# Attention phase of a two-layer decoder trunk: scores three head pairs ahead, turned rows in their own PSUM banks, a new order within each step

## The reference, cut to what matters

```python
D_MODEL, SEQ, HEAD_DIM, N_Q_HEADS, N_KV_HEADS, WINDOW, BLOCK = 1024, 4096, 64, 16, 4, 128, 128

# swa_sink_attention: blocks of 128 queries, each against its own and the preceding 128 keys
s = einsum('bnqkgd,bnjkd->bnkgqj', q, kb)              # q already scaled by HEAD_DIM ** -0.5
s = where(mask, s, -inf)                               # band of 128 keys
m = maximum(max(s, axis=-1), sink)
e = exp(s - m)
pr = e / (sum(e, axis=-1) + exp(sink - m))
o = einsum('bnkgqj,bnjkd->bnqkgd', pr, vb).reshape(B, S, N_Q_HEADS * HEAD_DIM)
h = h + o @ w_o
hn = rmsnorm(h, g_ffn[1])                              # rows for the experts
logits = hn @ [w_group_router, w_expert_router]        # 4 + 32 columns
```

## Time and profile before

| | |
|---|---|
| median of three runs | 5489.29 us |
| profiled execution, its own time | 5481.81 us |
| span of its trace | 5479.8 us |
| attention, first to last copy of `qT` | 2647.8 to 3562.2 us of the span |
| TensorE busy over the span | 4717.2 us (86%) |
| VectorE busy over the span | 2947.2 us (54%) |

### The profile page before, as it was taken

The page is one execution under the profiler, slowest core; times in us unless marked ns, Lnnn a source line. Parts: engine busy times, 40 slices in busy tenths (PEclk is TensorE's granted clock), DMA queues, the critical chain, the costliest instruction groups (busy, mean ns, idle before and its releaser), DMA issues. The chain is left out here.

```text
span 5479.8 us, 90667 instructions
## 1 busy us (share of the span) xinstructions
PE 4717.2 (86%) x29473; PEld 2996.9 (55%) x29893; DVE 2947.2 (54%) x5970; ACT 1945.8 (36%) x2841; POOL 1559.3 (28%) x1159
## 2 busy tenths in 40 slices
PE   7928999999938999998588888845999999986898
PEld 6916766666623444443355555524766676653444
DVE  5664444444444544443577777773444444435665
ACT  6714444433322122221344444413434344322232
POOL 1114444443401111110232333304444344322232
PEclk9959999999969999999799999967999999998999
DMA  6729999998945555553555555518999999854443
GB/s 219 273 96 316 308 308 302 302 295 285 288 139 143 147 146 143 153 146 93 130 146 153 149 148 151 140 46 277 307 309 304 297 310 282 289 162 150 146 137 114
DMA packets 1163421, 1129.77 MB, mean 206 GB/s; under 512 B 859984, under 2 KB 871248, under 8 KB 1163344
## 3 DMA queue, kind: packets, MB, share of 16 engines
q1 hardware_dynamic: 1117264, 961.02, 57.8%
q0 software_dynamic: 46080, 167.79, 9.4%
HBM read 695.58 MB, written 227.54 MB: 168 GB/s over the span
## 5 line engine op out<-in xcount | busy, mean ns | idle before, releaser
L724 POOL TENSOR_TENSOR ex_w_lo<-ex_raw,ex_w_hi 128x2048 bf16<-128x2048 f32 x192 | 779.2, 4085 | 1161.8 <-ACT ex_w_hi L778 1161.8
L778 ACT ACTIVATE ex_w_hi<-ex_raw 128x2048 bf16<-128x2048 f32 x384 | 707.3, 1900 | 523.4 <-PE ex_ps_y L110 187.9
L875 PE MATMUL ex_ps_gate<-ex_xT,ex_w_hi 128*128 128x0 bf16 x2048 | 572.3, 280 | 161.6 <-DMA ex_xT<-ex_xrow 126.3
L876 PE MATMUL ex_ps_gate<-ex_xT,ex_w_hi 128*128 128x0 bf16 x2048 | 572.1, 280 | 0.0
L877 PE MATMUL ex_ps_gate<-ex_xT,ex_w_lo 128*128 128x0 bf16 x2048 | 571.6, 279 | 0.0
L875 PE MATMUL ex_ps_up<-ex_xT,ex_w_hi 128*128 128x0 bf16 x2048 | 558.6, 273 | 0.0
L876 PE MATMUL ex_ps_up<-ex_xT,ex_w_hi 128*128 128x0 bf16 x2048 | 558.3, 273 | 0.0
L877 PE MATMUL ex_ps_up<-ex_xT,ex_w_lo 128*128 128x0 bf16 x2048 | 558.1, 273 | 0.0
L857 DVE COPY ex_y<-ex_ps_y 128x512 f32 x324 | 224.1, 692 | 566.5 <-PE ex_ps_y L110 515.6
L841 DVE TENSOR_TENSOR ex_aT<-ex_silu,ex_ps_up 128x384 bf16<-128x384 f32 x256 | 141.8, 554 | 719.6 <-PE ex_ps_up L877 538.2
L109 PE MATMUL ex_ps_y<-ex_w_lo,ex_aT 128*128 128x512 bf16 x1296 | 492.2, 380 | 8.5
(11 more groups left out here) (310 smaller groups left out, 9071.8 us busy)
## 6 DMA issues: line engine op xcount, KB each, us to landing
ex_raw<-in_w_exp_gate SPq DMA_DIRECT2D x128, 1024.0 KB, 11.1
ex_raw<-in_w_exp_up SPq DMA_DIRECT2D x128, 1024.0 KB, 13.8
ex_raw<-in_w_exp_down SPq DMA_DIRECT2D x128, 1024.0 KB, 5.8
y_rows<-ex_y SPq DMA_DIRECT2D x162, 512.0 KB
cb_hin<-h_mid SPq DMA_DIRECT2D x64, 512.0 KB, 4.7
mix_x<-in_x SPq DMA_DIRECT2D x32, 512.0 KB, 4.6
h_mid<-mix_h SPq DMA_DIRECT2D x32, 512.0 KB, 5.2
y_rows<-mix_zeros SPq DMA_DIRECT2D x32, 512.0 KB, 5.9
```

Of the source, the lines that this page charges most:

```text
L724: eng.tensor_tensor(w_lo[u][:, w], raw[:, c, :], w_hi[u][:, w], ALU.subtract).then_inc(lo_done, 1)
L778: act.activation(w_hi[u][:, c * WCHUNK:(c + 1) * WCHUNK], raw[:, c, :], ACT.Copy).then_inc(hi_done, 1)
L875: pe.matmul(out, hi, x_hi, start=j == 0, stop=False)
L876: pe.matmul(out, hi, x_lo, start=False, stop=False)
```

## The change: what it does

Times of issue are moved in all five lists; arithmetic, instruction counts and shapes stay.

- `scores`, `top`, `exps` are issued three pairs ahead (c + 3) in place of two. `ps_s` still has two halves.
- A new tile `ps_t` of two PSUM banks takes the turned queries, the turned `hn` rows and the logits. `ps_x` is left to the projection. The turned keys move to bank 0 of `ps_o`. `qT` is doubled.
- Queries and keys of tile s+1 are turned in slot 1 (before: slot 6).
- Square, scaling, power and `hn`: scaling and power of tile s-2 now stand in slot 0 and `hn` in slot 1 of step s (before: slots 6 and 7 of step s-1). Its PE transposes stand in slot 3, the copy `hnT` in slot 3, the router in slot 7.
- `project(0,0)` moves from slot 1 to slot 0, `project(1,0)` from 2 to 1, `project(.,1)` from 3 and 4 to 4 and 5.
- `over(s+1, 0)` moves ahead of the `top`s of slot 7; `rests` stood ahead of `over` in every slot already.
- SyncE: the `hrow` store moves from slot 1 to 5, the K/V load from 3 to 5, the `h4` store from 6 to 7.

```diff
-        qT = m.sb("qT", [P, NP, P])
+        qT = [m.sb(f"qT{u}", [P, NP, P]) for u in (0, 1)]
-        ps_log, ps_k = ps_o[:, 0, 0:NLOG], ps_o[:, 1, 0:2 * P].rearrange("p (j n) -> p j n", j=2)
+        ps_t = m.ps("t", [P, D])
+        ps_log, ps_k = ps_t[:, 0:NLOG], ps_o[:, 0, 0:2 * P].rearrange("p (j n) -> p j n", j=2)
...
 ScalarE
-                    if c < NP - 2 and cur:
-                        exps(s, c + 2)
+                    if c < NP - 3 and cur:
+                        exps(s, c + 3)
+                    if c >= NP - 3 and nxt:
+                        exps(s + 1, c + 3 - NP)
+                    if c == 1 and nxt:
+                        act.wait_ge(turn_mm, s + 2)
+                        wait(act, s_mm, NP * s)
+                        act.activation(qT[v][:], ps_t[:], ACT.Copy).then_inc(qT_done, 1)
+                    if c == 1 and prev2:
+                        act.wait_ge(hn_done, s - 1)
...
                         act.activation(hrow[u][:, 0:D], hn[:], ACT.Copy).then_inc(hi_done, 1)
                     if c == 2 and prev:
                         out_hi(s - 1, 1)
...
+                    if c == 3 and prev2:
+                        act.wait_ge(hnT_mm, s - 1)
...
+                        act.activation(hnT[:], ps_t[:], ACT.Copy).then_inc(hnT_done, 1)
+                    if c == 6 and cur:
+                        out_hi(s, 0)
                     if c == 6 and prev:
...
                         act.activation(junk[:], h4[v][:], ACT.Square, accum_out=ss[:]).then_inc(ss_done, 1)
...
 VectorE, after the change (rests, over as before)
                     if cur:
                         rests(s, c)
                     if c < NP - 1 and cur:
                         over(s, c + 1)
+                    if c == NP - 1 and nxt:
+                        over(s + 1, 0)
+                    if c == 0 and prev2:      # scaling of tile s-2
+                    if c == 1 and prev2:      # hn of tile s-2
+                    if c == 3 and prev:
+                        out_lo(s - 1, 1)
+                    if c == 4 and nxt:        # kT of tile s+1
+                    if c == 4 and cur:        # low part of the values
+                    if c == 3 and prev2:      # low part of hrow
+                    if c in (5, 6) and prev:
+                        residual(s - 1, v, c - 5)
+                    if c < NP - 3 and cur:
+                        top(s, c + 3)
+                    if c >= NP - 3 and nxt:
+                        top(s + 1, c + 3 - NP)
                     if c == 7 and cur:
                         out_lo(s, 0)
+                    if c == 7 and prev2:      # logits of tile s-2
...
 TensorE, after the change
+                    if c < NP - 3 and cur:
+                        scores(s, u, c + 3)
+                    if c == 5 and prev:
+                        project(1, 1).then_inc(wo_mm, 1)
+                    if c >= NP - 3 and nxt:
+                        scores(s + 1, v, c + 3 - NP)
+                    if c == 0 and prev:
+                        pe.wait_ge(ol_done, 2 * s - 1)
+                        wait(pe, h4_done, 2 * (s - 1))
+                        project(0, 0)
+                    if c == 1 and prev:
+                        project(1, 0)
+                    if c == 1 and nxt:        # turn queries into ps_t, keys into ps_k
+                    if c == 2 and prev:
+                        weigh(s - 1, v, 1)
+                    if c == 3 and prev2:      # turn hn into ps_t, after qT_done
+                    if c == 4 and prev:
+                        pe.wait_ge(ol_done, 2 * s)
+                        project(0, 1).then_inc(wo_mm, 1)
+                    if c == 6 and cur:
+                        weigh(s, u, 0)
+                    if c == 7 and prev2:      # router into ps_log
```

More of the change, by code:

```diff
@@ L1531, in step @@
                         turn(s, c)
-                    if c == 1 and prev2:
+                    if c == 5 and prev2:
                         sp.wait_ge(lo_done, s - 1)
                         sp.dma_start(row_t[s - 2], hrow[u][:]).then_inc(row_st[u], 16)
-                    if c == 3 and load:
+                    if c == 5 and load:
                         wait(sp, v_done, s + 1)
                         sp.dma_start(kv_in[u][:], kv_t[s + 2]).then_inc(kv_ld[u], 16)
-                    if c == 6 and prev:
+                    if c == 7 and prev:
                         sp.wait_ge(h4_done, 2 * s)
@@ L1562, in step @@
                 for c in range(NP):
[L1563 to L1566, removed]
                     if c < NP - 1 and cur:
@@ L1570, in step @@
                         heads(s + 1, 0)
+                    if c == 0 and prev2:
+                        pool.wait_ge(ms_done, s - 1)
+                        wait(pool, hn_done, s - 2)
+                        pool.tensor_tensor(rs[:], ms[:], C.minus_half[:], ALU.pow).then_inc(rs_done, 1)
             steps(pool, step)
@@ L1597, in step @@
                         act.activation(hrow[u][:, 0:D], hn[:], ACT.Copy).then_inc(hi_done, 1)
[L1598 to L1601, removed]
                     if c == 2 and prev:
                         out_hi(s - 1, 1)
-                    if c == 1 and cur:
+                    if c == 2 and cur:
                         act.wait_ge(kv_ld[u], done(s, u))
@@ L1609, in step @@
                         act.activation(vp[u][:, 0, :, :], vin, ACT.Copy).then_inc(vh_done, 1)
+                    if c == 3 and prev2:
+                        act.wait_ge(hnT_mm, s - 1)
+                        wait(act, log_mm, s - 2)
+                        act.activation(hnT[:], ps_t[:], ACT.Copy).then_inc(hnT_done, 1)
+                    if c == 6 and cur:
+                        out_hi(s, 0)
                     if c == 6 and prev:
                         act.wait_ge(h4_done, 2 * s)
-                        wait(act, ss_done, s - 1)
+                        wait(act, ms_done, s - 1)
                         act.activation(junk[:], h4[v][:], ACT.Square, accum_out=ss[:]).then_inc(ss_done, 1)
[L1614 to L1619, removed]
-                    if c < NP - 2 and cur:
-                        exps(s, c + 2)
-                    if c >= NP - 2 and nxt:
-                        exps(s + 1, c + 2 - NP)
             steps(act, step)
@@ L1678, in step @@
                 for c in range(NP):
-                    if c == 3 and prev:
-                        out_lo(s - 1, 1)
                     if cur:
@@ L1684, in step @@
                         over(s, c + 1)
[L1685 to L1696, removed]
+                    if c == NP - 1 and nxt:
+                        over(s + 1, 0)
+                    if c == 0 and prev2:
+                        dve.wait_ge(ss_done, s - 1)
+                        dve.tensor_scalar(ms[:], ss[:], 1.0 / D, EPS, ALU.mult, ALU.add).then_inc(ms_done, 1)
+                    if c == 1 and prev2:
+                        dve.wait_ge(rs_done, s - 1)
+                        wait(dve, hnT_mm, s - 2)
+                        dve.scalar_tensor_tensor(out=hn[:], in0=h4[u][:], scalar=rs[:, 0:1], in1=g_ffn[:],
+                                                 op0=ALU.mult, op1=ALU.mult).then_inc(hn_done, 1)
+                    if c == 3 and prev:
+                        out_lo(s - 1, 1)
+                    if c == 4 and nxt:
                         dve.wait_ge(turn_mm, s + 2)
@@ L1703, in step @@
                         last.then_inc(kT_done, 1)
[L1704 to L1714, removed]
+                    if c == 4 and cur:
+                        dve.wait_ge(vh_done, s + 1)
+                        vin = kv_in[u][:, KVW:2 * KVW].rearrange("p (j e) -> p j e", e=HEAD)
+                        dve.tensor_tensor(vp[u][:, 1, :, :], vin, vp[u][:, 0, :, :], ALU.subtract).then_inc(v_done, 1)
+                    if c == 3 and prev2:
                         dve.wait_ge(hi_done, s - 1)
@@ L1717, in step @@
                         dve.tensor_tensor(hrow[u][:, D:2 * D], hn[:], hrow[u][:, 0:D], ALU.subtract).then_inc(lo_done, 1)
+                    if c in (5, 6) and prev:
[4 more added lines that the diff above has]
+                        top(s + 1, c + 3 - NP)
                     if c == 7 and cur:
                         out_lo(s, 0)
[L1720 to L1724, removed]
+                    if c == 7 and prev2:
+                        dve.wait_ge(log_mm, s - 1)
+                        at = slice(s - 2, s - 1) if isinstance(s, int) else bass.ds(s - 2, 1)
+                        dve.tensor_tensor(C.logits[:, at, :].rearrange("p a b -> p (a b)"), ps_log, bias[:],
+                                          ALU.add).then_inc(log_done, 1)
             steps(dve, step)
@@ L1738, in scores @@
                 for b, keys in ((0, kT[1 - par]), (1, kT[par])):
-                    mm = pe.matmul(ps_s[:, c % 2, :, b * P:(b + 1) * P], qT[:, c, :], keys[:, jj, :, :],
```

(34 more changed lines are left out.)

4 lines of the change are left out of this document (1 added, 3 removed).

## The result

Four runs took 5327.07 to 5338.02 us, median **5332.57 us**; the kernel before, timed beside them, 5489.56. The ratio is 0.9716, 95% interval 0.9704 to 0.9728: 157 us faster, where 105 were forecast.

A forecast was written before the change was run, and what follows sets the result against it. TensorE is near its limit, VectorE second; a dependency circle of 26.0 us plus 0.4 for the clock gives steps of 26.4 against 29.9. Thirty steps save 105 us: 5384 us, range 5350 to 5440.

The forecast's parts named there:

- The wait for `hn` goes, the clock with it: TensorE's 2.8 us wait for `hn` ahead of its transposes goes; the clock's fall had cost 1.0 us a step.
- What is late next: `project(0,0)` in slot 0 waits about 2.2 us for `out_lo(s-1,0)`, at the end of a chain of 26.0 us.
- the circle: Chain from `project(0,0)` over scores, `top`, exponentials, `out_hi`, `out_lo`, slots 4 to 7 back to `project(0,0)`: 26.0 us.
- VectorE's own work, "a bare slot is ... in all 2.19": `rests` 0.79, `over` 0.25, `top` with `nmx` 1.15 make 2.19 us a slot; with the other work 23.9 a step.
- The clock, "I take 0.4": Clock falling at the new wait ahead of `project(0,0)` costs 0.4 us a step, within bounds of 0 and 2.6.
- TensorE's own work 23.85: Scores, `project`, `weigh`, router and transposes on TensorE sum to 23.85 us a step at 2.4 GHz.
- Filling and draining, "0, within 3": Steps outside the 30 counted have the same dependent chains: 0 us change, within 3 either way.
- Three ahead: `exps` gets over two slots before `over` wants it, where it had one, so VectorE's wait for it goes.
- SyncE: Moving the `hrow` store, K/V load and `h4` store costs 0, up to 1 us a step if a landing doubles.
- `over(s+1,0)`, "so 0": Moving it ahead of slot 7's last `top`s saves at most 1.15 us towards `heads`, 0 inside the loop.
- The exponentials' wait far below 9.7 us: Sign of being right: ScalarE's exponentials wait for `nmx` far below 9.7 us a step.
- A: Rival: TensorE runs through and the clock never falls, step 25.0 us at best, 5342 us; chance 0.13.

The follow-up runs named there:

- e4: Kernel before with only `hn` rows and logits given two PSUM banks of their own, `hn` turned in slot 2: 5384.22 us, 26.58 us a step.
- e2: Changed kernel with `out_lo(s,0)` moved from the end of slot 7 to behind `over` of the next slot 0: 5401.68 us, 27.30 us a step.
- e3: Changed kernel with `out_lo(s,0)` ahead of the last `top` of slot 7 and `out_hi(s,0)` ahead of slot 6's exponentials: 5312.13 us, 24.25 us a step.
- e9: Changed kernel with `residual(s-1,1)` in slot 7 in place of slot 6: 5333.66 us, 25.23 us a step in the mean.
- e10: Changed kernel with `over(s+1,0)` behind the last `top` of slot 7, as before the change: 5326.59 us, 24.88 us a step.
- e1: Changed kernel with `scores`, `top`, `exps` two pairs ahead in place of three, copy `kT` one slot later: 5407.40 us, 27.35 us a step.
- e7: Changed kernel with SyncE's order of `hrow` store, K/V load and `h4` store as before the change: 5329.21 us, 25.10 us a step.
- e6: e3 with the low part of `hrow` also moved from slot 3 to slot 2: 5320.52 us, 24.86 us a step.
- e8: e2 with the router's 16 narrow matmuls in slot 6 in place of slot 7: 5401.02 us, 27.3 us a step.

## Why the prediction was wrong, by its own steps

- *The wait for `hn` goes, the clock with it:* right. e4 shows it alone: 3.3 us a step.
- *What is late next:* right in place and order. TensorE's wait is where it was said, for `out_lo`; `out_lo` of slot 3 waits 0.86 for ScalarE. e2 and e3 moved the step at 2.4 GHz by +1.1 and -0.85, as the circle has it.
- *VectorE's own work, "a bare slot is ... in all 2.19":* **the step that failed.** The 2.19 was read from 3014.77 to 3016.96, a slot with nothing beside `rests`, `over` and `top`. It held 0.31 us without work: 0.17 ahead of `top` and 0.14 behind `nmx`, against the kernel after, where each follows its forerunner in 0.08. The lines of that slot that weren't read, from the kernel before:

```profile
3015.89 1.04 POOL L1558 TENSOR_TENSOR att_pr<-att_ex,att_rden 128x512 bf16<-128x512 f32 x1 [1.80 <-DVE att_rden L1651]
3016.74 0.21 DVE L1646 TENSOR_SCALAR att_nmx<-att_mx 128x2 f32<-128x2 f32 x1
```

`rests` at 3016.96 needs `heads`, which ends at 3016.93 and was released by `over` at 3015.56. So the slot is `rests` 0.79 and a round trip of 1.40 from `over` over GpSimd back to `rests`. It is 2.18 or 2.19 in every step of the loop before, though `top` begins 0.11 us behind `over` in half of them and 0.25 in the others: what is lost ahead of `top` is won back in the wait behind it. The prediction took the whole as VectorE's work and added each `residual` on top, though part of it fills the gap: slots 5 and 6 took 4.91, not 5.58. With `top` to `rests` 1.01 rather than 1.15 and slot 7 this is the 0.9 between 26.0 and 25.1: 27 us in thirty steps. The cause is shown for slot 6 by e9 and for slot 7 by e9 and e10; slot 5 has the same instructions as slot 6 and the same length, and was not tried.
- *The clock, "I take 0.4":* measured 0, another 12 us. It follows from the first error: the wait was 0.7 us, not 2.2. In e2 waits of 1.7 to 1.9 cost 1.1 a step (27.3 against 26.2), so at the forecast wait 0.4 would probably have been too little. That the two terms, 0.9 and 0.4, are wrong in the same direction is why the miss is so large.
- *TensorE's own work 23.85:* 24.25 (e3). Without effect on the time, as the circle is longer.
- *Filling and draining, "0, within 3":* 7 us less. The drain, last `heads` to last logits, is 3.1 shorter (30.9 to 27.8 us); the rest, some 4 us, lies in the first steps and was not looked into.
- *Three ahead; SyncE:* three ahead is worth 2.25 us a step in this order (e1, with the copy `kT` moved), more than its wait of `over`, since two ahead makes scores late too. SyncE 0, right (e7). `over(s+1,0)`, "so 0": it costs 0.22 (e10).
- *The exponentials' wait far below 9.7 us:* wrong, 276.1 us in 27 steps is 10.2. ScalarE has less than 15 us of work a step and simply waits for the next maxima; the sign to look for was VectorE's wait for `exps`, which is absent after (4.9 us a step before).
- *The rivals:* A's time (25.0, 5342) came nearest, for one of its reasons, the clock; scores to `top` stayed 1.31. Together: 27 + 12 + 7 us, 4 outside attention, and 2 by which the profiled execution lies nearer to its median than before. That is the 52 us missed.

## What to carry to other kernels

Before durations from a trace are added up along a chain, split each into work and waiting: a slot that looks bare may hold a wait on a third engine, and what is put into it then costs less than its own length (here 0.35 to 0.40 for 0.60). When a wait is removed from a hand-ordered loop, list every circle from an engine back to itself, not only the longest: here two and TensorE's own work lay within a us, and shortening one at the cost of another (e6) gave a longer step than e3. Look at each step of a loop before taking its mean: in e9 one step with a fall of the clock hid that the others hadn't changed. Look last for the instruction on which the busiest engine still waits; moving `out_lo` and `out_hi` by one place each gave 20 us more for no work.

## What the runs showed of the hardware

- VectorE and GpSimd hold each other up. `heads` takes 1.03 us beside `top` or a `residual`, and 2.00 where it starts inside `hn`; `nmx` takes 0.17 in most slots and up to 0.40 where a `heads` is still running, ending when `heads` ends. The Trainium skill (SBUF — State Buffer, Who interferes with whom) says that a VectorE instruction with two SBUF inputs contends with a GpSimd one that reads SBUF, and that copies and `tensor_scalar` can take both shared ports whole, so that the engine that comes second waits to the end of the other. Both rows agree.
- The granted clock fell in 18 of 24 steps at waits of 2.7 to 2.8 us with eight transposes behind them (before), in 12 of 24 at waits of 1.66 to 1.90 us (e2), in 9 of 24 at 2.1 to 2.65 us with the router moved away (e8), in 2 of 24 at 1.48 to 1.58 us (e1), in none at 0.65 to 0.72 us (after) and in one of 26 at 0.71 to 0.77 us (e9). In before, e2 and e8 waits of one and the same length had a fall in some steps and none in others.
